# Reordering four places of a hybrid attention/convolution/recurrence step: first load, window copies, first scores, first gathers

## What is computed

```
u = RMSNorm(h);  q, k/v of three branches, gates, conv and recurrence inputs = u @ w_in
prompt:  o_c, p = attention over compressed key blocks;  o_s = attention over the selected blocks
         o_w = banded attention, window 512
sample:  the same with paged caches: kc, vc = compress(cache pages + new);  top-k blocks by p
         ks, vs = pool[page_table] (4,096 old keys and values per sequence);  window buffer of 512
         win_k_s, win_v_s = last 512 rows of (old window buffer, new rows)     # outputs
h = h + RMSNorm(concat(attention, conformer, RG-LRU) @ w_out)
```

## Time and profile before

| what | value |
|---|---|
| median of 3 runs | 947.78 us (947.65 to 950.33) |
| the profiled execution | 957.26 us, its span 955.4 us |
| PE busy, share of the span | 896.9 us, 94% |
| DVE, ACT, POOL busy | 600.8, 371.0, 105.3 us |
| granted TensorE clock, mean | 0.978 of full |

### The profile page before, as it was taken

The page is one execution under the profiler, slowest core; times in us unless marked ns, Lnnn a source line. Parts: engine busy times, 40 slices in busy tenths (PEclk is TensorE's granted clock), DMA queues, the critical chain, the costliest instruction groups (busy, mean ns, idle before and its releaser), DMA issues.

```text
span 955.4 us, 16015 instructions
## 1 busy us (share of the span) xinstructions
PE 896.9 (94%) x6261; PEld 573.2 (60%) x6261; DVE 600.8 (63%) x1129; ACT 371.0 (39%) x844; POOL 105.3 (11%) x105
## 2 busy tenths in 40 slices
PE   6999999999999999997999999997885999999997
PEld 4656665666666666665667776775643666544443
DVE  4698879999789887976465666566632444322221
ACT  4312262110113001135887787766633656411111
POOL 0012100000010111101002202120240230000000
PEclk9999999999999999998999999999897999999999
DMA  8435542412144366542600000000135988532111
GB/s 298 162 132 179 196 154 58 60 59 67 44 139 161 110 208 206 207 202 61 235 2 2 2 2 2 2 2 2 45 135 240 353 301 328 213 122 88 70 52 55
DMA packets 32110, 118.34 MB, mean 124 GB/s; under 512 B 3433, under 2 KB 11771, under 8 KB 22971
## 3 DMA queue, kind: packets, MB, share of 16 engines
q0 software_dynamic: 9360, 68.16, 19.6%
q1 hardware_dynamic: 19053, 43.39, 12.9%
q10 hardware_dynamic: 3623, 5.76, 2.9%
HBM read 108.33 MB, written 13.29 MB: 127 GB/s over the span
## 4 chain that ended last, share of the span: by engine, by line
PE 76%; DVE 8%; DMA 7%; ACT 3%; DVEq 2%; issue 2%; POOL 1%; ACTq 0%; SPq 0%; POOLq 0%
PE PS L833 26%; PE PS L2038 12%; PE PS L1587 6%; PE PS L1577 6%; DMA main<-in_cmp_v_dram,row 5%; PE PS L1605 5%; PE PS L809 3%; PE PS L1889 3%; PE PS L1868 3%; PE PS L1900 2%; DVE main L606 2%; PE PS L1555 2%; PE PS L1923 2%; ACT main L1397 2%; DMA main<-in_sel_k_dram,row 2%
## 5 line engine op out<-in xcount | busy, mean ns | idle before, releaser
L833 PE MATMUL PS<-main 128*128 128x352 f32 (+1 forms) x1056 | 331.5, 473 | 0.0
L833 PEld LDWEIGHTS PS<-main 128*128 128x128 f32 x1056 | 202.2, 192 | 121.3 <-issue 4.4
L1397 ACT ACTIVATE main<-PS,main 128x512 f32<-128x512 f32 (+3 forms) x192 | 103.9, 562 | 43.3 <-DVE main L1426 21.0
L2038 PE MATMUL PS<-main 128*128 128x512 f32 x256 | 112.3, 593 | 0.1
L434 ACT ACTIVATE main<-PS 128x384 f32<-128x384 f32 x24 | 11.8, 491 | 210.2 <-PE PS L833 204.0
L644 DVE SCALAR_TENSOR_TENSOR main<-main,par 128x1022 f32<-128x1022 f32 (+16 forms) x66 | 83.9, 1271 | 5.3 <-issue 0.4
L603 DVE TENSOR_TENSOR main<-main 128x1024 f32<-128x1024 f32 x64 | 75.5, 1221 | 16.2 <-DMA main<-in_cmp_v_dram,row 10.4
L2038 PEld LDWEIGHTS PS<-main 128*128 128x128 f32 x256 | 47.6, 190 | 56.4 <-issue 56.4
L1587 PE MATMUL PS<-cst,main 128*128 128x128 f32 x528 | 73.5, 288 | 8.3 <-ACT main L1397 8.2
L606 DVE TENSOR_TENSOR main<-main 128x1024 f32<-128x1024 f32 (+2 forms) x96 | 75.0, 781 | 7.2
L1389 ACT ACTIVATE main<-PS 128x512 f32<-128x512 f32 (+1 forms) x138 | 69.7, 597 | 18.3 <-PE PS L1587 18.1
(11 more groups left out here) (317 smaller groups left out, 1029.5 us busy)
## 6 DMA issues: line engine op xcount, KB each, us to landing
main<-in_w_tiles_dram SPq DMA_DIRECT2D x24, 512.0 KB, 3.6
out_dram<-main SPq DMA_DIRECT2D x18, 256.0 KB, 2.1
main<-in_x_prompt_dram SPq DMA_DIRECT2D x8, 512.0 KB, 9.2
main<-in_w_out_dram SPq DMA_DIRECT2D x4, 1024.0 KB, 5.9
main<-in_x_prompt_dram SPq DMA_DIRECT2D x16, 256.0 KB, 2.9
out_dram<-main SPq DMA_DIRECT2D x4, 512.0 KB
diag<-in_win_k_dram SPq DMA_DIRECT2D x8, 256.0 KB, 7.3
diag<-in_win_v_dram SPq DMA_DIRECT2D x8, 256.0 KB, 7.3
```

Source lines behind the costliest of these rows:

```text
L833: last = pe.matmul(bank(3 * s + j)[:, 0:w], ring[:, s, k * P:(k + 1) * P], xT[:, k, t0:t0 + w], start=(k == 0), stop=(k == KD - 1))
L1397: last = act.activation(prob[:, k % 2, g, h * nk_ * P:(h + 1) * nk_ * P], score_set(k, g)[:, h * nk_ * P:(h + 1) * nk_ * P], ACT.Exp, scal ...
L2038: last = pe.matmul(out_bank(m, h), proj[:, MIX[k], n * P:(n + 1) * P], wo[:, k, h * 512:(h + 1) * 512], start=(x == 0), stop=(x == KD - 1))
```

## The change

Four places change.

- The first tile of x is loaded ahead of the constants.
- The two copies of the old window rows are issued behind the natural stores, no longer ahead of them.
- PE computes the scores of the first batch ahead of the prompt turn. The turn writes to banks 4 to 7, since the scores are in 0 to 3, and DVE, no longer ACT, copies it out, behind its first four peaks. ACT's first exponential waits for the turn (`cmp_pt_ps`).
- `pool_decode` issues keys and values of a half in turn, keys first, also in the first round.

```diff
         def sp_startup(sp):
-            sp.dma_start(cst[:, :], dram["constants"]).then_inc(ld_cst, 16)
             for n in range(3):
                 sp.dma_start(xn[:, n, :], dram["x_prompt"][n * P:(n + 1) * P, :]).then_inc(ld_x[n], 16)
+                if n == 0:
+                    sp.dma_start(cst[:, :], dram["constants"]).then_inc(ld_cst, 16)
...
         def sp_natural(sp):
-            for k, key in enumerate(("win_k", "win_v")):
-                sp.dma_start(outs[11 + 2 * k][0, :, 0:WIN - DS].rearrange("b w g d -> b w (g d)"), dram[key][:, DS:, :]).then_inc(out_done, 16)
             wait_natural(sp)
...
+            for k, key in enumerate(("win_k", "win_v")):
+                sp.dma_start(outs[11 + 2 * k][0, :, 0:WIN - DS].rearrange("b w g d -> b w (g d)"), dram[key][:, DS:, :]).then_inc(out_done, 16)
...
             for k in range(2 * NT):
-                last = pe.transpose(bank(0, 4)[:, k * P:(k + 1) * P], sc[:, k * P:(k + 1) * P], ident)
+                last = pe.transpose(bank(4, 4)[:, k * P:(k + 1) * P], sc[:, k * P:(k + 1) * P], ident)
             last.then_inc(SEM["cmp_pt_ps"], 1)
 
-        def act_prompt_turn(act):
-            act.wait_ge(SEM["cmp_pt_ps"], 1)
+        def dve_prompt_turn(dve):
+            dve.wait_ge(SEM["cmp_pt_ps"], 1)
             flat = ptc.rearrange("p i g q -> p (i g q)")
             for h in range(2):
-                act.activation(flat[:, h * T:(h + 1) * T], bank(2 * h, 2), ACT.Copy)
-            act.drain().then_inc(SEM["cmp_pt"], 1)
+                dve.tensor_copy(flat[:, h * T:(h + 1) * T], bank(4 + 2 * h, 2))
+            dve.drain().then_inc(SEM["cmp_pt"], 1)
...
                 for g in range(G):
                     act.wait_ge(SEM["s_max"], 2 * k + g + 1)
+                    if k == 0 and g == 0:
+                        act.wait_ge(SEM["cmp_pt_ps"], 1)
...
             for k in BATCH[0]:
                 peak(k)
+            dve_prompt_turn(dve)
...
         def pe_pairs(pe):
-            pe.wait_ge(SEM["cmp_pt"], 1)
-            for h in range(2):
-                pe.wait_ge(taken[(M_VN + h) % 2], (M_VN + h) // 2 + 1)
-            pe.wait_ge(SEM["vb_ready"], 1)
...
+            natural_free(pe, 6)
+            natural_free(pe, 7)
             for k in BATCH[0]:
                 scores(k)
+            for h in range(2):
+                pe.wait_ge(taken[(M_VN + h) % 2], (M_VN + h) // 2 + 1)
+            pe_prompt_turn(pe)
+            pe.wait_ge(SEM["vb_ready"], 1)
+            pe.wait_ge(SEM["cmp_pt"], 1)
...
         def pool_decode(pool):
             pool.wait_ge(SEM["oz"], NT)
             pool.wait_ge(SEM["nat_out"], 16 * N_NAT)
-            for h in range(2):
-                pool_values(pool, 0, h)
             for rnd in range(4):
                 for h in range(2):
                     if rnd < 3:
...
                         pool_keys(pool, rnd + 1, h)
                     if rnd >= 1:
                         pool.wait_ge(SEM["vused"], 2 * (rnd - 1) + h + 1)
-                        pool_values(pool, rnd, h)
+                    pool_values(pool, rnd, h)
```

More of the change, by code:

```diff
@@ L2178, in _ @@
             act_natural(act)
-            act_prompt_turn(act)
             act_branch_a_gates(act, 3, 4)
@@ L2293, in _ @@
             pe_natural(pe)
-            pe_prompt_turn(pe)
             pe_pairs(pe)
```

## The result

The changed kernel takes 940.01 us (median of five, 938.73 to 942.38), the kernel before, run beside it, 950.10 us (947.65 to 951.02). The ratio is 0.9896, 95% interval 0.9875 to 0.9918: 9.9 us faster, where 15.5 were predicted, and just above the upper end of the range (939.5). The profiled execution of the changed kernel took 939.83 us, span 938.0, mean granted clock 0.987. It lies in the middle of its timed runs, while that of before (957.26) lies 6 us above the highest of its own. The two spans therefore differ by 17.4 us, the timed runs by 9.9. Of all timed executions in this document one, the last of e4, took 1108.41 us at a mean granted clock of 0.806, where the others had 0.976 to 0.996; it stands in no ratio.

The account below looks back on a forecast made before the run. PE was taken to bound the kernel, with 76% of the chain of waits. Middle 5.3, gathers 10.2 and first load 0 sum to 15.5 us, off the median of 947.78: 932.3 us, range 929 to 939.5.

Parts of the forecast that it names:

- the middle stretch: From the late compressed-value gather to the fifth batch's scores: copies and first scores together gain 5.3 us, between 3 and 6.1.
- Gathers, 10.2 us: Beginning of decode: with keys issued first, PE's 9.74 us wait for them goes, to within 1 us; gain 10.2 us.
- Keys come no earlier: Rival in decode: gathers of one burst all end together, so only the middle counts, 942.5 us; chance 0.04.
- another wait in decode: Rival: values of h = 0 or keys of h = 1 arrive late, losing 3 to 6 us, 935 to 938; chance 0.12.
- Copies: Before the masks: the late gather lands in time, PE's 3.31 us idle and the slow clock go; 5.5 us earlier.
- First scores: First batch: with scores ahead of the turn, PE reaches the second batch's scores 4.5 to 7.7 us earlier in all.
- The cap: DVE's `part_out` waits for the natural stores, landing 5.6 us earlier, at 464.1; the middle can keep at most 6.1 us.
- the middle gives nothing back: Rival: DVE's copies, the table load and the stores' landing leave only 0 to 2.5 us, 935 to 938; chance 0.11.
- Nothing gives the lead back: From the middle to decode, PE, ACT and DVE programs are unchanged and wait only for each other: no loss.
- First load, 0 us: Startup: loading x's first tile earlier gives a lead ending at the sixth tile; 0 us, between 0 and 1.
- Shared transfers (slower): Rival: window copies among the natural stores delay their landing by 16 us or more, up to 960.5 us; chance 0.05.
- The base: The median of the timed runs of the kernel before, 947.78 us, from which 15.5 us were taken to give 932.3.

Follow-up runs that it names:

- e4: The kernel before with only the first scores moved ahead of the prompt turn, which DVE copies out; 953.29 us, ratio 1.0025.
- e13: The changed kernel with the old order of POOL's gathers in decode, the other three places kept; 947.50 us, ratio 0.9963 to the kernel before.
- e1: The kernel before, with nothing edited, timed and profiled again; 951.22 us, ratio 1.0000.
- e6: The changed kernel with the prompt turn ahead of the first scores again, copied by ACT; 937.39 us, ratio 0.9855 to the kernel before.
- e17: The changed kernel with PE's first turn waiting for DVE's first copy alone and ACT's table loaded early; 942.47 us, ratio 0.9911 to the kernel before.
- e15: The changed kernel with round 0's key gathers held until the stores land, the turn's copy split and ACT's table loaded early; 931.99 us, ratio 0.9810.
- e14: The kernel before with only the window copies moved behind the natural stores, a repeat of e3; 948.44 us, ratio 0.9973.
- e3: The kernel before with only the window copies moved behind the natural stores; 948.69 us, ratio 0.9979.
- e8: The kernel before with only the first tile of x loaded ahead of the constants; 951.03 us, ratio 1.0001.

## Why the prediction was wrong, step by step

The measured gain is below the forecast by 7.7 us, 940.01 instead of 932.3, which is 0.5 us outside the range. Three amounts make it up, told below: the term of the middle stretch was mis-sized, 5.3 us where the runs give 3.5 (1.8 us); the median from which I subtracted was low (2.3 us); and 3.6 us stay open. Without any one of them the time would have been in the range.

**Gathers, 10.2 us: right as a part alone.** Alone 10.5 us; in the traces 10.56 us from POOL's first gather to the mark in round 1. The orders, the landings in time, PE's new limit by ACT (waits of 0.50 and 0.25 us where I had foreseen ACT) are as worked out. "Keys come no earlier" and "another wait in decode" are refuted. In the changed kernel they seem to be worth less: it is faster than e13, which lacks only this place, by 6.2 to 8.8 us (0.9963 against 0.9896, 0.9870, 0.9898). In the traces the span behind POOL's first gather is 9.6 us shorter on average with the new order (239.3 us in eleven profiles against 249.0 in nine).

**Copies: mechanism right, size from the wrong execution.** The late gather lands in time and the idle time is gone. But I let PE "use its whole 3.31". With the copies in their old place, eight profiles show idle times before L1270 of 3.31, 1.27, 2.78, 1.55, 1.71, 3.08, 1.66 and 1.88 us, mean 2.2. The sum was made from the largest. The copies' 5.5 us became 2.3 in timed runs. Also, up to the second scores 13 windows of 1 us are below full clock in the first profile, 5 in e1.

**First scores: the steps of the path right, their worth not.** Turn, two copies by DVE (2.36 us for two, 2.56 foreseen), 2.52 us of idle time (2.7 foreseen), the slow turn (3.47 us, 3.9 foreseen): the second scores come 10.8 us earlier, 6.2 of it behind the projection, inside my 4.5 to 7.7. But then the cap took it.

**The cap: seen, and set too high. This is the step that failed.** I wrote that the stores land "5.6 us earlier too, at 464.1, and no more", which keeps their 22.6 us from first issue to landing as they were, and that PE may keep 6.1 us; my sign was a wait of `part_out` of 2 to 4 us. The wait is 5.06 us (4.10 to 6.09 in the other profiles of the changed program). The stores took 23.8 us and started 0.4 us later than foreseen, with the projection's end as zero; `part_out` ended its wait 4.0 us earlier and not 5.6, and the fifth scores came 4.0 us earlier even against the untypical first profile, 3.3 us against the mean of the four. e13 gives the whole stretch 3.5 us in timed runs (1.9 to 5.1), where I had 5.3. The traces say the same, and where it went: in the four executions of the changed program the first store is issued 15.3 us after the projection and the stores take 23.4, in the four with copies and scores in their old place 19.3 and 22.9. That is 4.0 us earlier, of which I had 5.6 because I took the stall of the first profile, the largest, off in full; less 0.5 us of longer landing, which I had at nothing: 3.5. The rival "the middle gives nothing back" named this wait; half of it came true. What I had not drawn from the rows: the last store's landing is set by the DMA engines' load, gathers included, so the stretch is bounded by a transfer and not by PE. With that bound a faster first batch is worth nothing that the timing shows (e6, e17).

The Trainium skill ("DMA: Bandwidth & Descriptors", section "Queues, rings and completion order") says that each DMA engine takes turns between the queues that have work for it, a packet at a time. The runs fit this, 12.2 to 12.3 us without the gathers' queue and 22.6 to 24.2 with it; that the turns go by packets no run here shows.

**"Nothing gives the lead back": wrong by 0.35 us.** From the fifth scores to a late side product (L1555, the last 66 to 69 us ahead of POOL's first gather) every execution takes 162.7 us without the first scores moved and 163.05 with them, or some 1.65 us more per stretch at the lower clock; PE idles 1.62 us there instead of 1.25. With the turn's copy split (e15, e17) it is 162.7 and 1.25 us again, so the loss hangs on how the copy and the table load were placed and not on the scores' move itself.

**First load, 0 us: right in worth, wrong in reason.** The lead does not end at the sixth tile; at the end of the projection 0.4 us may be left of it, which neither the traces' scatter nor the timing tells from none.

**Shared transfers (slower): refuted.** With the copies behind the stores, and the scores in their old place, these land 22.6 (e6), 22.7 (e14) and 23.2 us (e3) after the first is issued; with both in their old place it is 22.6, 22.7, 22.8 and 23.4 (e8). What shared the engines with the stores were the key gathers, which stood beside them before the change too.

**The base.** I took 15.5 us off the median of three, 947.78. The median of five beside the changed kernel is 950.1, those of the later runs are 950.3 to 952.3. That alone is 2.3 us of the 7.7 that I missed; the middle's size is 1.8. What remains, 3.6 us, is the largest of the three and is not settled: the parts add up to 10.5 + 3.5 = 14.0 us, the changed kernel, timed three times, shows 9.9, 12.4 and 9.7. Intervals of 1.6 to 2.8 us to either side on each leave room for chance. A candidate, only argued: with the keys' stall in place, slow stretches of PE ahead of it cost nothing, since the keys' landing follows POOL's start; without the stall they cost 1.6 us each. The spans behind POOL's first gather fit this in part: 248.5 to 249.8 us with the old order of gathers, 237.6 to 241.4 with the new one.

## What to carry to other kernels

Before summing the pieces of one profiled execution, compare its time with the timed runs: if it lies above them, as here by 6 us, some of its stalls may be samples from the long end (3.31 us against a mean of 2.2), and a second profile of the same kernel shows which. When a buffer's release hangs on a DMA, work out what else loads the DMA engines until it lands; speeding up compute ahead of it only lengthens the wait, while moving the competing transfers (here key gathers that nobody needs for 250 us) makes the compute gain real: on the changed kernel (0.9870 to 0.9898) late keys give 0.9856, the split copy 0.9911, both 0.9810. And a wait for two copies where the next step needs only the first is worth splitting when it stands in a short idle time of PE.

## What the runs showed of the hardware that was not expected

Identical stretches of PE's program differ between executions in steps, not smoothly: from the same late side product of PE (L1555) to POOL's first gather 66.6 to 66.7 us in seven profiles and 68.3 to 68.4 in the thirteen others, the longer ones with one more stretch, or two, at a granted clock of 0.50 in the windows. An idle time of 2 to 3 us of PE is followed by such a stretch in one execution and not in another of the same kernel, as with the 2.05 us in e1 (scores in 1.99 us) and the first profile (3.11 us), or the 2.52 us in e13 (turn in 2.35 us at full clock) and in the changed kernel (3.47 us), whose programs are the same up to there. The Trainium skill ("TensorE: Matmul & The Clock Gate", section "Part 1: The HAM clock gate (the "warmup" mystery)") says that the count of slow matmuls at a kernel's start varies from run to run; these rows show the like in the middle of a kernel, where it is worth 1.65 us each time. And four gathers of 1 MB beside 12 stores nearly doubled the stores' time to land, from 12.2 or 12.3 to 22.6 us and more.
